# A step of a hybrid backbone on one core: the experts of layer 1 sorted by load into places of different size

## The reference, cut to what matters

```
def moe_swiglu(h, router, w1, w3, w2):
    probs = softmax(h @ router)                     # 8 experts
    top_p, top_i = top_k(probs, 2); top_p /= sum(top_p)
    gates = one_hot(top_i) * top_p, summed over the two
    for e in range(8):                              # w1, w3: 1024 x 1408, w2: 1408 x 1024
        y += gates[:, e] * ((silu(h @ w1[e]) * (h @ w3[e])) @ w2[e])
```

## Time and profile before

| | us |
|---|---|
| median of 3 runs | 2710.22 (2710.1 to 2718.47) |
| profiled execution | 2724.16 |
| its span | 2722.3 |
| PE busy | 2521.7 (93%) |
| DVE busy | 1401.3 (51%) |
| ACT busy | 1128.5 (41%) |
| mean granted clock | 0.975 |

### The profile page before, as it was taken

One profiled execution on the slowest core, in us unless ns is written; L12 is line 12 of the kernel. 1 busy time (PEld: TensorE's weight loads), 2 busy tenths in 40 slices (PEclk: granted clock), 3 DMA queues, 4 the chain that ended last, 5 costly groups with the idle time before them and its releaser, 6 DMA issues.

```text
span 2722.3 us, 68039 instructions
## 1 busy us (share of the span) xinstructions
PE 2521.7 (93%) x30324; PEld 2197.1 (81%) x30324; DVE 1401.3 (51%) x2474; ACT 1128.5 (41%) x2126; POOL 146.1 (5%) x163
## 2 busy tenths in 40 slices
PE   6998799898899999989987999998999999999996
PEld 3996577676798999969965777766899999999995
DVE  2337455556533333362374665474565555555565
ACT  3226544544421211242255545444444444444452
POOL 0002000010000000010010010001000000000011
PEclk8999899999999999999998999998999999999998
DMA  7223023320122222222200222202765666566672
GB/s 273 78 78 127 24 74 96 96 75 27 70 77 72 78 78 78 72 72 78 78 11 1 66 66 66 65 5 109 240 209 178 214 212 207 183 211 211 181 259 83
DMA packets 82701, 304.58 MB, mean 112 GB/s; under 512 B 9376, under 2 KB 9504, under 8 KB 82272
## 3 DMA queue, kind: packets, MB, share of 16 engines
q1 hardware_dynamic: 71072, 257.93, 29.6%
q0 software_dynamic: 11328, 42.21, 4.2%
HBM read 273.11 MB, written 27.00 MB: 110 GB/s over the span
## 4 chain that ended last, share of the span: by engine, by line
PE 83%; DVE 8%; issue 3%; ACT 3%; DMA 1%; POOL 0%; SPq 0%; another core or an unknown queue 0%; DVEq 0%; ACTq 0%; POOLq 0%
PE ps L451 19%; PE ps L452 19%; PE ps L453 19%; PE ps L1183 7%; PE ps L812 3%; PE ps L917 2%; PE ps L464 2%; PE ps L1115 2%; PE ps L960 1%; PE ps L976 1%; DMA ring<-in_blocks 1%; PE ps L463 1%; DVE arena L2474 1%; DVE arena L2473 1%; PE ps L1167 1%
## 5 line engine op out<-in xcount | busy, mean ns | idle before, releaser
L2278 DVE TENSOR_TENSOR ring_lo<-ring,w_ffn 128x1024 fp32r<-128x1024 f32 x264 | 322.5, 1225 | 214.5 <-ACT w_ffn L1702 208.5
L451 PE MATMUL ps<-hg_hi,w_ffn 128*128 128x256 f32 x1408 | 402.5, 286 | 3.2 <-DVE hg_lo L2909 3.2
L452 PE MATMUL ps<-hg_lo,w_ffn 128*128 128x256 f32 x1408 | 398.0, 283 | 0.0
L453 PE MATMUL ps<-hg_hi,ring_lo 128*128 128x256 f32 x1408 | 397.5, 282 | 0.0
L1702 ACT ACTIVATE w_ffn<-ring 128x1024 fp32r<-128x1024 f32 x264 | 278.1, 1057 | 197.7 <-PE ps L453 196.2
L451 PEld LDWEIGHTS ps<-hg_hi,w_ffn 128*128 128x128 f32 x1408 | 267.4, 190 | 4.8 <-DVE hg_lo L2909 3.4
L452 PEld LDWEIGHTS ps<-hg_lo,w_ffn 128*128 128x128 f32 x1408 | 266.5, 189 | 1.2
L453 PEld LDWEIGHTS ps<-hg_hi,ring_lo 128*128 128x128 f32 x1408 | 267.0, 190 | 0.0
L1183 PEld LDWEIGHTS ps<-arena 64*64 64x64 f32 x7680 | 165.0, 135 | 98.1 <-issue 78.5
L453 PE MATMUL ps<-hT_ffn_hi,ring_lo 128*128 128x320 f32 x704 | 216.0, 307 | 0.0
L1183 PE MATMUL ps<-arena 64*64 64x64 f32 x7680 | 190.5, 222 | 22.6 <-issue 22.2
(11 more groups left out here) (375 smaller groups left out, 5107.1 us busy)
## 6 DMA issues: line engine op xcount, KB each, us to landing
ring<-in_blocks SPq DMA_DIRECT2D x484, 512.0 KB, 3.7
h_rows<-arena POOLq DMA_DIRECT2D x16, 512.0 KB, 10.2
arena<-h_rows POOLq DMA_DIRECT2D x7, 1024.0 KB, 9.9
y_rows<-arena POOLq DMA_DIRECT2D x7, 1024.0 KB, 6.6
...
out_y_all<-x POOLq DMA_DIRECT2D x5, 512.0 KB, 3.7
...
```

Of the source, the lines that this page charges most:

```text
L451: nc.tensor.matmul(dst, w_hi, m_hi, start=start, stop=False)
L452: nc.tensor.matmul(dst, w_hi, m_lo, start=False, stop=False)
L453: return nc.tensor.matmul(dst, w_lo, m_hi, start=False, stop=stop)
L2278: V.tensor_tensor(ring_lo[:, n % RING, :], ring[:, n % RING, :], high[:, n % high.shape[1], :], ALU.subtract).then_inc(*E.sig("w_lo"))
```

## The change

The experts are ranked by load. Rank r gets `RANK_CAP[r]` slots: 256, 240, 208, 192, 176, 160, 144, 128. They are worked through in eight places that take the ranks 0, 6, 1, 5, 2, 4, 3, 7, so the places have 256, 144, 240, 160, 208, 176, 192 and 128 slots, fixed in the program; which expert stands in a place is known only when the ranks are. DVE works that out and stores eight expert numbers; SP loads them in eight registers before it issues the first block of the stage, and each of the stage's 264 block reads takes its address from one. The second program part is entered when an expert has more than its place holds.

With it the up-projection is written anew: the high part of a block multiplies the high and the low parts of the tokens in one matmul of 2n columns (n the place's slots), the low part the high ones in one of n. The two halves of a PSUM bank (4, 5 and 6 in turn, one for each block) are added by a TENSOR_REDUCE on DVE before anything reads them. Three slots of `w_ffn` stay; the high part of block b + 3 is made when b is used. The down-projection takes the tiles that a place has (one in the last, two in the others, the second one partly filled); transposes, evictions, stores and the last selection follow the sizes, and the transposes use one bank (7) where there were two. PE, ACT and DVE load the value of the branch after place 0, not before it.

```
+RANK_CAP = [256, 240, 208, 192, 176, 160, 144, 128]
+RANK_AT = [0, 6, 1, 5, 2, 4, 3, 7]
+CAPS = [RANK_CAP[r] for r in RANK_AT]
+Y_AT = [sum(CAPS[:p]) for p in range(NE)]
...
+        def slots(k):
+            return CAPS[k] if k < NE else CAP
...
+        def up_bank(f, w):
+            return 4 + (2 * f + w) % 3
+        def up_at(f, w):
+            return 2 * f + w + max(0, f - 1)
+        def up_before(k, f, w):
+            return 2 * FE * k + 2 * f + w
+        def halves(bank, n):
+            return ps[:, bank, 0:2 * n].rearrange("p (h n) -> p h n", h=2)
+        def summed(bank, n):
+            return ps[:, bank, 0:2 * n].rearrange("p (h n) -> p n h", h=2)
+        u_sum, v_sum = ftmp[:, 0, CAP:2 * CAP], ftmp[:, 1, CAP:2 * CAP]
...
+            expert = []
             for n in range(N_BLOCKS):
+                if n == MOE_FIRST:
+                    sp.wait_ge(sem["rt_rank"], 2)
+                    expert = [sp.value_load(flag_i[0:1, 1 + p:2 + p], min_val=0, max_val=NE - 1) for p in range(NE)]
                 if n >= RING:
 
                     sp.wait_ge(sem["block_used"], n - RING + 1)
-                sp.dma_start(ring[:, n % RING, :], blocks[n]).then_inc(ring_sem[n % RING], 16)
+                if n < MOE_FIRST:
+                    sp.dma_start(ring[:, n % RING, :], blocks[n]).then_inc(ring_sem[n % RING], 16)
+                else:
+                    p, c = divmod(n - MOE_FIRST, EXP_B)
+                    sp.dma_start(ring[:, n % RING, :], blocks[bass.ds(expert[p] * EXP_B + (MOE_FIRST + c), 1)].rearrange("n p d -> p (n d)")).then_inc(ring_sem[n % RING], 16)
...
             def up(k, f):
 
-                hi, lo = hg(k)
-                if f >= 2:
-                    pe.wait_ge(sem["eh_lo"], hidden_before(k) + f - 1)
+                m, n = hg(k), slots(k)
                 for w in range(2):
+                    if 2 * f + w >= 3:
+                        pe.wait_ge(sem["up_ev"], up_before(k, f, w) - 2)
                     w_h, w_l = split_blk(w_ffn)
+                    both = halves(up_bank(f, w), n)
                     for kc in range(KC):
                         c = slice(kc * P, (kc + 1) * P)
-                        mm = mm_split(nc, ps[:, 4 + f % 2, w * CAP:(w + 1) * CAP], w_h[:, c], w_l[:, c], hi[:, kc, :],
-                                      lo[:, kc, :], kc == 0, kc == KC - 1)
+                        nc.tensor.matmul(both, w_h[:, c], m[:, :, kc, 0:n], start=kc == 0, stop=False)
+                        mm = nc.tensor.matmul(both[:, 0, :], w_l[:, c], m[:, 0, kc, 0:n], start=False, stop=kc == KC - 1)
                     done(mm)
...
-                for s in range(2):
-                    slots = slice(s * P, (s + 1) * P)
+                for s, rows in tiles(k):
+                    r = slice(s * P, s * P + rows)
                     for h in range(2):
                         half = slice(h * 512, (h + 1) * 512)
-                        mm = mm_split(nc, ps[:, 2 * s + h, :], ge_hi[:, g % 2, slots], ge_lo[:, g % 2, slots], w_h[:, half],
...
-                    flag = flag_of(pe)
                     for e in range(NE):
                         moe_expert(e)
+                        if e == 0:
+                            flag = flag_of(pe)
...
+            def hidden(k, f, more):
+                first, n = FFN_AT[1] + k * EXP_B, slots(k)
+                w_hi(w_ffn, first + up_at(f, 0) + 3)
+                act.wait_ge(sem["up_ev"], up_before(k, f, 0) + 1)
                 if f >= 2:
-                    act.wait_ge(sem["eh_lo"], hidden_before(k) + f - 1)
-                A(ftmp[:, f % 2, 0:CAP], ps[:, 4 + f % 2, 0:CAP], ACT.Tanh, scale=0.5).then_inc(*E.sig("eh_th"))
-                for n in ahead(f)[0]:
-                    w_hi(w_ffn, first + n)
+                    act.wait_ge(sem["eh_g"], hidden_before(k) + f - 1)
+                A(ftmp[:, f % 2, 0:n], u_sum[:, 0:n], ACT.Tanh, scale=0.5).then_inc(*E.sig("eh_th"))
+                if more or f < FE - 1:
+                    w_hi(w_ffn, first + up_at(f, 1) + 3)
                 act.wait_ge(sem["eh_g"], hidden_before(k) + f + 1)
-                A(ge_hi[:, f % 2, :], ftmp[:, f % 2, CAP:2 * CAP], ACT.Copy).then_inc(*E.sig("eh_hi"))
-                for n in ahead(f)[1]:
-                    w_hi(w_ffn, first + n)
+                A(ge_hi[:, f % 2, 0:n], v_sum[:, 0:n], ACT.Copy).then_inc(*E.sig("eh_hi"))
+                if f >= 1 and (more or f < FE - 1):
+                    w_hi(w_ffn, first + up_at(f, 1) + 4)
...
-                V.tensor_reduce(rstat[:, 16:17], ps[:, 1, 40:48], AX.X, ALU.max).then_inc(*E.sig("dve_step"))
+                V.scalar_tensor_tensor(key, ps[:, 1, 40:48], float(NE), C("iota")[:, 0:NE], ALU.mult, ALU.subtract).then_inc(*E.sig("dve_step"))
                 dve.wait_ge(*E.own_last())
+                V.tensor_tensor(above, key.unsqueeze(1).broadcast_to([P, NE, NE]), key.unsqueeze(2).broadcast_to([P, NE, NE]), ALU.is_gt).then_inc(*E.sig("dve_step"))
                 V.tensor_scalar(rk, rk, -1.0, None, ALU.add).then_inc(*E.sig("rt_rank"))
-                V.tensor_copy(flag_i[0:1, 0:1], rstat[0:1, 16:17]).then_inc(*E.sig("rt_rank"))
-                dve.wait_ge(sem["rt_rank"], 2)
-                select(0, 0, 0, 0)
+                dve.wait_ge(*E.own_last_of("dve_step"))
+                V.tensor_reduce(rank, above, AX.X, ALU.add).then_inc(*E.sig("dve_step"))
+                dve.wait_ge(*E.own_last())
+                V.tensor_tensor(place, rank.unsqueeze(2).broadcast_to([P, NE, NE]), C("rank_at").unsqueeze(1).broadcast_to([P, NE, NE]), ALU.is_equal).then_inc(*E.sig("dve_step"))
+                dve.wait_ge(sem["rt_rank"], 1)
+                dve.wait_ge(*E.own_last())
+                at_place(mtmp, rk, 0)
+                V.tensor_tensor(ptmp[:, 0], place, C("iota")[:, 0:NE].unsqueeze(2).broadcast_to([P, NE, NE]), ALU.mult).then_inc(*E.sig("dve_step"))
+                V.tensor_tensor(ptmp[:, 1], place, C("caps").unsqueeze(1).broadcast_to([P, NE, NE]), ALU.mult).then_inc(*E.sig("dve_step"))
+                dve.wait_ge(*E.own_last())
+                V.tensor_reduce(eid, ptmp[:, 0].rearrange("p e q -> p q e"), AX.X, ALU.add).then_inc(*E.sig("dve_step"))
+                V.tensor_reduce(rstat[:, 20:25], mtmp, AX.X, ALU.add).then_inc(*E.sig("dve_step"))
+                V.tensor_reduce(cap_e, ptmp[:, 1], AX.X, ALU.add).then_inc(*E.sig("dve_step"))
+                dve.wait_ge(*E.own_last())
+                V.tensor_copy(flag_i[0:1, 1:1 + NE], eid[0:1, :]).then_inc(*E.sig("rt_rank"))
+                for i in range(NT):
+                    V.tensor_scalar(sel0[:, i, :], C("iota"), 1.0, rstat[:, 20 + i:21 + i], ALU.add, ALU.is_equal).then_inc(*E.sig("sel_dve" if i == NT - 1 else "dve_step"))
+                V.tensor_tensor(over_e, ps[:, 1, 40:48], cap_e, ALU.subtract).then_inc(*E.sig("dve_step"))
+                V.tensor_tensor(ptmp[:, 0], place, C("iota")[:, 0:NE].unsqueeze(1).broadcast_to([P, NE, NE]), ALU.mult).then_inc(*E.sig("dve_step"))
+                V.tensor_tensor(ptmp[:, 1], place, C("y_at").unsqueeze(1).broadcast_to([P, NE, NE]), ALU.mult).then_inc(*E.sig("dve_step"))
+                dve.wait_ge(*E.own_last())
+                V.tensor_reduce(y_base, ptmp[:, 1], AX.X, ALU.add).then_inc(*E.sig("dve_step"))
+                V.tensor_reduce(rstat[:, 16:17], over_e, AX.X, ALU.max).then_inc(*E.sig("dve_step"))
+                V.tensor_reduce(pos, ptmp[:, 0], AX.X, ALU.add).then_inc(*E.sig("dve_step"))
+                dve.wait_ge(*E.own_last())
+                V.tensor_scalar(flag_i[0:1, 0:1], rstat[0:1, 16:17], float(CAP), None, ALU.add).then_inc(*E.sig("rt_rank"))
                 for i in range(2, NT):
                     x_lo(htok_lo0[:, i, :], htok[:, i, :], htok_hi[:, i, :])
                 places()
                 w_lo(w_ffn, FFN_AT[1])
+            def at_place(dst, ranks, p):
+                V.scalar_tensor_tensor(dst, ranks, 1.0, place[:, :, p].unsqueeze(1).broadcast_to([P, NT, NE]), ALU.add, ALU.mult).then_inc(*E.sig("dve_step"))
...
+            def hidden(k, f, more):
+                first, n = FFN_AT[1] + k * EXP_B, slots(k)
+                t, u, v = ftmp[:, f % 2, 0:n], u_sum[:, 0:n], v_sum[:, 0:n]
+                dve.wait_ge(sem["block_used"], first + up_at(f, 0) + 1)
+                V.tensor_reduce(u, summed(up_bank(f, 0), n), AX.X, ALU.add).then_inc(*E.sig("up_ev"))
+                w_lo(w_ffn, first + up_at(f, 0) + 3)
+                dve.wait_ge(sem["block_used"], first + up_at(f, 1) + 1)
+                dve.wait_ge(sem["eh_lo"], hidden_before(k) + f)
+                V.tensor_reduce(v, summed(up_bank(f, 1), n), AX.X, ALU.add).then_inc(*E.sig("up_ev"))
                 dve.wait_ge(sem["eh_th"], hidden_before(k) + f + 1)
-                b = ps[:, 4 + f % 2, :]
-                t, g = ftmp[:, f % 2, 0:CAP], ftmp[:, f % 2, CAP:2 * CAP]
-                V.scalar_tensor_tensor(t, t, 1.0, b[:, 0:CAP], ALU.add, ALU.mult).then_inc(*E.sig("dve_step"))
```

(14 more changed lines are left out.)

199 lines of the change are left out of this document (99 added, 100 removed).

## The result

The changed kernel takes 2605.8 us (median of 4 runs, 2597.4 to 2613.6), the one before on the same chip 2714.3 (4 runs): a ratio of 0.960, 95% interval 0.956 to 0.964. The profiled executions are 2607.3 and 2724.2 us long; their spans differ by 2722.3 - 2605.5 = 116.8 us, where the medians differ by 108.5: the profiled execution of the kernel before is 10 us longer than its median, and no profile here shows where.

What follows compares the result with a forecast made beforehand. TensorE was taken to bound the kernel; stage -102, start +12, flag load +1 and end -2 make -91 on the profiled 2724.16, or 2633; the median, 14 us lower, gives 2620 us (own range 2598 to 2642, whole range 2594 to 2678).

Steps and rivals of the forecast that it cites:

- What bounds the stage: Expert stage: TensorE bounds it, so each microsecond of its work removed is worth a microsecond until another engine is late.
- the price of a pair: Up-projection: a block's wide and narrow matmul together cost 0.350 us at 256 slots, falling to 0.231 at 128.
- TensorE's gain of 102 + 15 us: Expert stage: 102 us less in up-projections, 15 us less in the last place's single-tile down-projection; -117 us in total.
- the floor: Up-projection: a load and narrow matmul take at least 0.112 us; without it TensorE's total would be -135 us.
- What VectorE gives back, 15 us: Last place: VectorE-bound, gives back about 20 us less the little others do; the stage gains 102 us instead of 117.
- The start, +12 us: Stage's start: SP waits for the ranking, so first blocks and gather evictions come later; +12 us, bounds +3 and +25.
- Flag load +1: Between places 0 and 1: loading the branch value stops PE for 0.49 us and its checks; +1 us.
- End -2: After the last down-projection: one tile of slots means fewer evictions, low parts and combine matmuls; -2 us.
- A: Rival, up-projection: f32r matmuls under 256 columns lose their pace; 2850 us at four times (0.09), 2677 at two (0.03).
- D: Rival: an expert overflows its place, so the second program part of 16 passes runs; 4100 us, called excluded by the slots.
- B: Rival: VectorE or hand-overs bound all small places; 2646 us, up to 2670 with late low parts; chance 0.09.
- C: Rival: the start costs 25 us or more as transfers share full DMA engines; 2635 to 2645 us, chance 0.05.

Runs made afterwards that it cites:

- the run at 240 columns: Changed kernel with the low part's matmul streaming 240 columns (120 high, 120 low) in every place; ratio 0.957 to the kernel before, stage 660.5 us.
- fixed addresses: Changed kernel with the experts' order as constants in SP's block reads, no wait for the ranking and no register loads; ratio 0.958 to the kernel before.

## Why the prediction came out as it did

**What bounds the stage, and the price of a pair: right.** The gain on the profiled execution was forecast as 91 us and is 116.8; the mechanism is the one named, and each piece of the difference is a size. The time forecast for the median, 2620 us with its own range of 2598 to 2642, holds 2605.8 in part by luck: the medians differ by 108.5 us, and a gain of 116.8 off the 2710.22 would have been 2593.

**TensorE's gain of 102 + 15 us: right.** Pair by pair the prices hold within 0.002 us, with the floor (the run at 240 columns). By columns alone the up-projections would have gained 134 us for 102 and the whole 149; the prediction's 135 for the whole leaves out the 15 of the down-projection, and its two figures for a stage without the floor, 121 us and the 2594 at the end of the range, don't fit each other.

**What VectorE gives back, 15 us: too much, the first mis-sized term.** The stage gained 116.3 us for 102. The last place was to take 76 us and took 69.2; the seven others were 0.1 to 2.4 us shorter than worked out, 673 to 658.5 over all eight. By the prediction's own prices TensorE's work in these seven (pairs, 2.77 us of down-projection a tile, transposes) is an estimated 94.2, 75.8, 90.5, 78.2, 85.6, 80.7 and 82.1 us, which is what they last within 0.5 us but for the 1.8 at 144 slots: what the hand-overs were to add on top wasn't there. In the last place VectorE gives back 13 us over TensorE's 56, not 20; that the stage still gains as much as TensorE's work does is since the 9.3 us of waits went too. The reduce was priced right (0.68 and 0.42 us predicted, 0.69 and 0.42 measured). In the last place what was wrong is how operations were strung together: durations were added, 67 us, with 0.1 us for each handing over on top. The trace has 62.0 busy us there and starts nearer together than the durations say (6.99 for 7.42 us a tile). The Trainium skill ("VectorE: DVE Perf Modes", in the section on two Vector instructions with no wait between them) says that a held instruction starts only when every earlier one has finished, so that one that isn't held needn't wait for that. The rows agree: starts lie up to 0.09 us ahead of the end before them.

**The start, +12 us: wrong, the step that failed.** It is +3.3 to the first up-projection (up to +4.8 in the other profiles with this start). To the end of the first place it is 121.5 us for 122.6; that has some 2.6 us of gain of the new loop in it (the run with seven places of 256), so about 1.5 of the start's cost are left there, by that estimate. The numbers were stored 2.4 us after the ranks (2.6 predicted), SP issued 4.8 us later for 6.4 (behind the first of the eight loads they start 0.55 us apart, where 0.77 was taken), the first block landed 3.5 us on, and blocks 1 and 2 at 1.6 us intervals behind it, not late. The first gather eviction came 15.8 us after the ranks for 20.2. Then the two holes in the gather before didn't come back: 11.5 us from first eviction to first up-projection for 15.3. The prediction named that as its lower bound, +3, and took +12. It also took the clock to be at half speed there in both. That holds for the gather, but not at its end. The same stretch before the change, and after:

```profile
1908.00:1912.00 4.00, 1.17 (x5) 1.17 (x6) 1.98 (x4) 0.66 (x2) 0.91 (x1) 0.50 0.97 373
```

```profile
1908.00:1912.00 4.00, 3.58 (x30) 3.38 (x29) 1.73 (x4) 1.54 (x4) 0.73 (x1) 1.00 1.03 420
```

Before the change the half clock reaches into the first up-projections (1908 to 1915 us, behind the last hole), and the first expert lasts 1.8 us longer than the next; now it is over at 1907. The step's mechanism isn't refuted: SP released 9.0 us later costs 12.9 us, and with the gather written ahead of the weights the first up-projection comes 23.0 us after the ranks, sooner than the 24.1 before the change.

What made the two holes before is open. TensorE's are put to "issue" (2.24 us) and to VectorE (3.16), ScalarE's second one to no engine. With fixed addresses the second came back (4.38 us on TensorE), the first hardly. An early gather with full DMA engines isn't enough for them: the run that gathers ahead of the first weights has both (first eviction 10.7 us after the ranks, a DMA share of 1.03 from 1900 to 1905 us), and TensorE waits for 0.7 us at most in its gather and for 1.5 behind it. In the two kernels with the second hole a 16 KB packet of the instruction queue starts inside it, at 1908.0 and 1903.6 us; in the changed kernel it starts at 1913.9, outside the gather. Whether that is the cause no run here shows.

**Flag load +1: hidden.** TensorE is busy for 92.87 of the 93 us up to the end of the first place, with its load of the flag (at 2003.80) among them, and goes from one place to the next without a stop (2006.39, 2006.63). **End -2: right** (-2.2).

**Rivals.** A falls by the pairs, D by the stage's length. B is true of the last place alone; with a single tile it would be of the place of rank 6 too. C has its mechanism shown and its price not reached.
